# Branch norms, silu and output projection moved from the u half to the v half of a two-layer decoder trunk

## What is computed

```python
mod = (c_act @ w_ada[l] + b_ada[l])[:, None, :]
sh1, sc1, g1, sh2, sc2, g2 = jnp.split(mod, 6, axis=-1)
h = rms_norm(x) * (1.0 + sc1) + sh1
q, k, v, qi, ki, wi, cu = jnp.split(h @ w_in[l], offs, axis=-1)
attn = dsa_attention(q, k, v, qi, ki, wi).reshape(B, T, ATTN_WIDTH)   # q, k, qi, ki normed, with rope
conv = conformer_conv(cu, ...)          # GLU -> conv of 31 taps -> layer_norm -> silu
mixed = jnp.concatenate([rms_norm(attn, out_g_attn[l]), rms_norm(conv, out_g_conv[l])], axis=-1)
x = x + g1 * (mixed @ w_out[l])
h2 = rms_norm(x) * (1.0 + sc2) + sh2
# peer: q = h2 @ w_q; top 16 experts e of 16384 per token and head; coef = softmax(scores) * gelu(u[e] . h2)
x = x + g2 * sum(coef * v[e])
```

## Time and profile before

| | us |
|---|---|
| median of 3 runs | 1897.99 |
| lowest and highest | 1894.2, 1899.7 |
| the profiled execution | 1898.82 |
| its span in the trace | 1896.8 |

### The profile page before, as it was taken

How to read it: one execution, slowest core, us unless ns; L and a number is a source line. 1 busy time by engine, 2 the same in 40 slices (tenths; PEclk the granted TensorE clock), 3 DMA queues, 4 the chain that set the end, 5 groups by cost and what they waited for, 6 DMA issues and landing times.

```text
span 1896.8 us, 20984 instructions
## 1 busy us (share of the span) xinstructions
PE 1071.0 (56%) x7558; PEld 630.1 (33%) x7558; DVE 1042.1 (55%) x2867; ACT 300.3 (16%) x851; POOL 976.5 (51%) x1072
## 2 busy tenths in 40 slices
PE   3896840784786566755486555774477550003554
PEld 2584630653462115443254114453153110000110
DVE  2312399799538018888518307789728219993000
ACT  6222100243210002342100002352010000000000
POOL 2000044553355776445435677534556777776774
PEclk8897975897797667876688787986788885556887
DMA  8547798999999999999999999997999999999998
GB/s 289 176 136 267 266 369 329 382 400 343 360 336 400 409 409 402 397 388 348 401 400 402 408 409 406 399 396 277 401 405 380 409 409 410 410 410 406 407 409 321
DMA packets 230920, 696.15 MB, mean 367 GB/s; under 512 B 23958, under 2 KB 23974, under 8 KB 230818
## 3 DMA queue, kind: packets, MB, share of 16 engines
q0 software_dynamic: 148080, 538.24, 72.5%
q1 hardware_dynamic: 82738, 156.58, 22.7%
HBM read 693.70 MB, written 1.05 MB: 366 GB/s over the span
## 4 chain that ended last, share of the span: by engine, by line
DMA 40%; PE 24%; DVE 14%; POOL 11%; issue 5%; ACT 5%; POOLq 0%; ACTq 0%; DVEq 0%
DMA rows<-in_peer_v,v_at 18%; DMA rows<-in_peer_u,u_at 8%; DMA wring<-in_w_in 8%; POOL rows L517 7%; PE ps L652 6%; DVE rows L1116 6%; PE ps L599 5%; PE ps L610 5%; POOL rows L509 4%; DMA wring<-in_w_ada 4%; ACT rows L907 2%; PE ps L575 2%; PE ps L633 1%; DMA wring<-in_w_out 1%; ACT diag_eq L907 1%
## 5 line engine op out<-in xcount | busy, mean ns | idle before, releaser
L509 POOL DMA_INDIRECT rows<-in_peer_u,u_at x512 | 480.6, 939 | 585.6 <-DVE dots L1116 254.2
L1116 DVE CUSTOM_DVE_ANT_0 rows<-rows,ps 128x1024 f32<-128x1024 f32 x512 | 601.6, 1218 | 224.5 <-DMA rows<-in_peer_u,u_at 217.0
L517 POOL DMA_INDIRECT rows<-in_peer_v,v_at x512 | 484.5, 946 | 313.2 <-PE ps L652 155.4
L652 PE MATMUL ps<-rows,spread_c 128*32 128x512 f32 x2048 | 343.9, 804 | 260.8 <-DMA rows<-in_peer_v,v_at 259.6
L599 PE MATMUL ps<-wring,hT 128*128 128x512 f32 x384 | 206.0, 692 | 74.9 <-DMA wring<-in_w_in 48.3
L652 PEld LDWEIGHTS ps<-rows,spread_c 128*32 128x32 f32 x2048 | 73.8, 129 | 504.0 <-issue 500.1
L610 PE MATMUL ps<-hT,wring 128*128 128x128 f32 x1536 | 184.5, 284 | 7.3 <-ACTq L874 7.3
L610 PEld LDWEIGHTS ps<-hT,wring 128*128 128x128 f32 x1536 | 182.2, 200 | 11.2 <-ACTq L874 8.5
L599 PEld LDWEIGHTS ps<-wring,hT 128*128 128x128 f32 x384 | 81.9, 222 | 187.2 <-issue 93.9
L907 ACT ACTIVATE diag_eq<-ident,cwT 128x128 f32<-128x128 f32 x395 | 118.3, 387 | 28.9 <-PE ps L633 27.5
L548 PE MATMUL ps<-ident,coef 128*128 128x128 f32 x4 | 1.5, 373 | 192.4 <-DVE coef L1384 192.4
(11 more groups left out here) (193 smaller groups left out, 959.8 us busy)
## 6 DMA issues: line engine op xcount, KB each, us to landing
wring<-in_w_ada SPq DMA_DIRECT2D x48, 1024.0 KB, 11.4
wring<-in_w_in SPq DMA_DIRECT2D x48, 1024.0 KB, 22.3
wring<-in_peer_wq SPq DMA_DIRECT2D x32, 1024.0 KB, 12.7
wring<-in_w_out SPq DMA_DIRECT2D x16, 1024.0 KB, 19.6
rows<-in_peer_u,u_at POOLq DMA_INDIRECT x512, 12.8
rows<-in_peer_v,v_at POOLq DMA_INDIRECT x512, 9.1
wring<-in_w_in SPq DMA_DIRECT2D x4, 288.0 KB, 23.7
out_x<-xs SPq DMA_DIRECT2D x2, 512.0 KB, 4.7
```

The lines of the kernel that those rows point to most:

```text
L509: pool.indirect_dma_start(row(n), None, u_rows, bass.IndirectOffsetOnAxis(ap=u_at[:, p % 2, k:k + 1], axis=0)).then_inc(row_landed[n % SLO ...
L517: pool.indirect_dma_start(row(n), None, v_rows, bass.IndirectOffsetOnAxis(ap=v_at[:, p % 2, tok:tok + 1], axis=0)).then_inc(row_landed[n % ...
L652: ins = pe.matmul(ps[32 * g:32 * g + 32, YB + q, :], spread_c[:, g, a, :], row(n)[:, q * 512:q * 512 + 512], start=a == 0, stop=a == 31)
L1116: dve.tensor_tensor_reduce(out=row(n), in0=row(n), in1=h2_shown, scale=1.0, scalar=0.0, op0=ALU.mult, op1=ALU.add, accum_out=dots[:, k:k + ...
```

## The change

The output projection with all that leads to it goes from `first(p)` to `second(p)` on every engine. On DVE `first(p)` now ends with the division of the attention values; a new function `join(p)` at the head of `second(p)` does the conv norm (p > 0), the attention branch's norm, waits for the silu and does the conv branch's norm. For p > 0 ScalarE copies the conv bank to `hb` at the place where the silu stood, and the conv norm reads that copy. ScalarE's silu and its evacuation of `mT` come at the head of its `second`. PE takes `coefT` and the first two steps of the sums ahead of the join's turn, and has three more steps around the two output blocks and one ahead of the turn of h2; so each query block finds 4 more steps done. The order of the weight loads stays. For p = 0 the conv norm stays where it was and the order of the two branch norms is swapped.

```diff
         ada(p, "mix")
+        if p:
+            job("coefT", p - 1)
         for q in range(2):
             job("mT", p, q)
...
         ada(p, "out")
-        if p:
-            job("coefT", p - 1)
@@ PE, first(p)
-                pe.wait_ge(mixed_ready, p + 1)
-                for q in range(2):
-                    turn4(("mT", p, q), [hb[:, (4 * q + i) * P:(4 * q + i + 1) * P] for i in range(4)])
-                pe.wait_ge(mixedT_ready, 2 * (p + 1))
-                for b in range(2):
-                    proj(("out", p, b), hT)
-                ada(p, "out")
@@ PE, second(p)
-                v_to(p - 1, 1)
+                v_to(p - 1, 2)
+                pe.wait_ge(mixed_ready, p + 1)
+                for q in range(2):
+                    turn4(("mT", p, q), [hb[:, (4 * q + i) * P:(4 * q + i + 1) * P] for i in range(4)])
+                pe.wait_ge(mixedT_ready, 2 * (p + 1))
+                for b in range(2):
+                    proj(("out", p, b), hT)
+                    v_to(p - 1, 3 + b)
+                ada(p, "out")
+                v_to(p - 1, 5)
                 pe.wait_ge(h2_ready, p + 1)
...
-                v_to(p - 1, 2)
+                v_to(p - 1, 6)
...
-                    v_to(p - 1, 4 + 2 * b_)
+                    v_to(p - 1, 8 + 2 * b_)
@@ ScalarE, first(p)
                 if p:
-                    silu()
+                    act.wait_ge(conv_full, p + 1)
+                    act.copy(hb[:, AW:D], ps[:, CONV_BANK, :]).then_inc(conv_taken, 1)
...
+            def second(p):
+                l, t = divmod(p, 2)
+                act.wait_ge(silu_in, p + 1)
+                act.activation(hb[:, AW:D], hb[:, AW:D], ACT.Silu).then_inc(silu_done, 1)
                 for q in range(2):
                     evac_scaled(("mT", p, q), q, mixedT_ready, gcol)
@@ DVE, first(p)
                 if p:
-                    conv_norm()
                     more_dots(3)
...
                 if p == 0:
-                    conv_norm()
-                dve.wait_ge(silu_done, p + 1)
-                rsqrt(half_mean_square(hv, CW, gy[:, :]), 1)
-                seq_(ts(hv, hv, rs[:, 0:1], None, ALU.mult))
+                    conv_norm(0)
...
-                rsqrt(half_mean_square(ha, AW, gy[:, :]), 1)
-                seq_(ts(ha, ha, rs[:, 0:1], None, ALU.mult), mixed_ready)
@@ DVE, new; second(p) calls it first
+            def join(p):
+                if p:
+                    conv_norm(p)
+                for n, cols in enumerate((slice(0, AW), slice(AW, D))):
+                    if n:
+                        dve.wait_ge(silu_done, p + 1)
+                    rsqrt(half_mean_square(hb[:, cols], AW, gy[:, :]), 1)
+                    seq_(ts(hb[:, cols], hb[:, cols], rs[:, 0:1], None, ALU.mult), mixed_ready if n else None)
```

More of the change, by code:

```diff
@@ L987, in first @@
                         evac(("skT", p, n), skT[:, 4 * n:4 * n + 4, :].rearrange("p g n -> p (g n)"), skT_ready)
-                def silu():
-                    act.wait_ge(silu_in, p + 1)
-                    act.activation(hb[:, AW:D], hb[:, AW:D], ACT.Silu).then_inc(silu_done, 1)
                 if p:
-                    silu()
+                    act.wait_ge(conv_full, p + 1)
+                    act.copy(hb[:, AW:D], ps[:, CONV_BANK, :]).then_inc(conv_taken, 1)
                 ns = CHUNKS[t]
@@ L1014, in first @@
                 ada(p, "mix")
-                if p == 0:
-                    silu()
+            def second(p):
+                l, t = divmod(p, 2)
+                act.wait_ge(silu_in, p + 1)
+                act.activation(hb[:, AW:D], hb[:, AW:D], ACT.Silu).then_inc(silu_done, 1)
                 for q in range(2):
@@ L1019, in first @@
                 ada(p, "out")
-            def second(p):
-                l, t = divmod(p, 2)
                 for q in range(2):
@@ L1276, in first, with conv_norm @@
                         rinv[:, :].unsqueeze(2).to_broadcast([P, NH, DH]), ALU.mult), pv_taken)
-                rsqrt(half_mean_square(ha, AW, gy[:, :]), 1)
-                seq_(ts(ha, ha, rs[:, 0:1], None, ALU.mult), mixed_ready)
+            def conv_norm(p):
+                hv = hb[:, AW:D]
+                if p == 0:
+                    dve.wait_ge(conv_full, 1)
+                    o = ps[:, CONV_BANK, :]
+                else:
+                    dve.wait_ge(conv_taken, p + 1)
+                    o = hv
+                seq_(dve.bn_stats(bn6[:, :], o))
+                seq_(dve.bn_aggr(mv[:, :], bn6[:, :]))
+                rsqrt(ts(halfv[:, 0:1], mv[:, 1:2], 0.5, 0.5 * NORM_EPS, ALU.mult, ALU.add), 1)
+                seq_(ts(hv, o, mv[:, 0:1], rs[:, 0:1], ALU.subtract, ALU.mult), None if p else conv_taken)
+                seq_(tt(hv, hv, ln_gb[:, 0, :], ALU.mult))
+                seq_(tt(hv, hv, ln_gb[:, 1, :], ALU.add), silu_in)
+            def join(p):
[6 more added lines that the diff above has]
+                    seq_(ts(hb[:, cols], hb[:, cols], rs[:, 0:1], None, ALU.mult), mixed_ready if n else None)
             def best16(lists):
@@ L1363, in second @@
                 l, t = divmod(p, 2)
+                join(p)
                 dve.wait_ge(g1_ready, 2 * (l + 1))
```

## The result

| | median us | lowest, highest |
|---|---|---|
| before | 1898.85 (4 runs) | 1894.2, 1901.67 |
| after | 1870.58 (4 runs) | 1867.49, 1875.68 |

The ratio is 0.9848, with a 95% interval of 0.9831 to 0.9865: 28 us faster, where 32 were forecast (1866). A second set of runs of the changed kernel, on the chip of three experiments, gave 0.9862 (0.9827 to 0.9898). The profiled execution of after took 1869.38 us, its span 1867.6.

What follows compares the result with a forecast made beforehand. The DMA stream of gathered rows bounds from 240 us on, with DVE behind u-half holes, and a serial chain before. Gains 3.7 + 22.6 + 3.2 + 2.9 = 32.4 us off 1898.82 gave 1866; range 1852 to 1890.

Steps and rivals of the forecast that it cites:

- The holes as the only place to win: From 240 us on, time can be won only where the DMA stream is not full: 45 us within reach.
- DVE's 7.8 us in each u half: u halves, p = 1 to 3: norms moved away give back 7.8, 7.0 and 7.8 us, sum 22.6.
- p = 0: Serial chain before the first gather: division and attention norm come inside the silu wait, 3.7 us gained, bounds 2 and 4.
- what follows the coefficients: After coefficients, v half: 3.2 us gained in p = 1, 0 in p = 2, 2.9 in p = 3.
- the first projection block: Half of the output projection's pair, between steps 1 and 2 of the sums: 7.4 to 8.5 us.
- the slower rival: v half projection runs at PE's lower clock, pair 29.6 us, 13 us lost per part: 1906 us, chance 0.09.
- no change: Projection's pause takes back the u half's gain, three new holes of 9.6 us: 1898 us, chance 0.08.
- the signs of being wrong: u halves' holes keep length, stream under 300 GB/s between second and third sum in all parts, or pair over 20 us.
- The pause: v half, between steps 1 and 2 of the sums: 15 to 19 us, against 16.5 us of ring.
- Selection: Path from coefficients to h2 grows some 11 us in p = 2 and 3; PE stands 8 to 11; cost nothing.
- the margin of 3 us: Spare cover of the ring (16.5 us) over PE's stand at the turn of the expert numbers: 3 us at least.
- ScalarE at nothing: Silu and table load leave the u half, a copy of about 0.6 us replaces them: costs nothing.

Runs made afterwards that it cites:

- Experiment b: Kernel before with conv norm, silu and both branch norms left out for p = 1 to 3, PE's order kept; 1883.09 us, ratio 0.9916.
- g: Changed kernel with conv norm, silu and branch norms left out for p = 1 to 3; 1868.13 us against 1874.78 for the changed kernel beside it.
- h: Changed kernel with 14 more products (10 us) on DVE ahead of the join for p = 1 to 3; 1899.44 us, ratio 0.9988.
- e: Changed kernel without ScalarE's copy, the conv norm reading the conv's PSUM bank; 1868.09 us, ratio 0.9827 to the kernel before.
- j: Changed kernel with the join for p = 2 and 3 back late in the u half, 6 dots after the division; 1872.74 us, ratio 0.9858.
- c: Kernel before with PE's new order alone, norms and silu staying in the u half; 1893.30 us, ratio 0.9951.

## Why the prediction was right, and by how much not

*The holes as the only place to win: held.* 24.6 of 28 to 29 us are filled holes, some 22 in the second trace. The mean from the first gather on is 396 GB/s; 397 was said, and 390 was before.

*DVE's 7.8 us in each u half: held as a sum.* 7.2, 6.0 and 7.3 us against 7.8, 7.0 and 7.8; in the second trace 3.9, 7.2 and 8.6. That is 20.5 and 19.7 against 22.6. The coefficients of p = 1, said to come near 488, come at 488.0 and 492.8. Experiment b shows the cause, and that in p = 2 it needs the new order of PE, which the prediction did not see: it summed the two parts as if independent.

*p = 0: 3.0 against 3.7.* The step itself was sized right: from the silu's release to the joined block 2.8 us (173.82 to 176.58) where it was 6.5.

```profile
173.82 0.69 DVE L1079 CUSTOM_DVE_ANT_0 gy<-hb 128x512 f32<-128x512 f32 x1 [14.47 <-ACT hb L1018]
...
176.10 0.49 DVE L1285 TENSOR_SCALAR hb<-hb,rs 128x512 f32<-128x512 f32 x1
```

The block was ready 5 us earlier in all, since the silu also came 1.2 us earlier in this execution; part of it was given back further on, in a stretch that PE crossed at the lower clock (window 202 to 212, granted 0.50; 1.00 before).

*The term that was mis-sized is what follows the coefficients.* In p = 1 I charged a hole of 5 us and 2.5 was there (3.9 in the second trace), so 5.7 us gained and not 3.2. In p = 2 and 3 I charged nothing and found 1.3 and 1.6, and at 1430 to 1450, where I had 2.9 gained, 1.3. One reason is the first projection block, costed at 7.4 to 8.5 us: it took 9.76, 8.83 and 9.94, the second 7.13 each time. That speaks for the small holes of p = 2 and 3; in p = 1 the block was longer than said and the hole smaller all the same, so there the estimate of what the ring and the weights still bring was too low. The granted clock of p = 1 in the first 5 us of the first block and in the rest of it:

```profile
503.76:508.76 5.00, 5.00 (x6) 2.18 (x7) 0.00 (x0) 0.00 (x0) 0.00 (x0) 0.50 1.03 405
508.76:513.50 4.74, 4.74 (x15) 1.78 (x17) 0.00 (x0) 0.00 (x0) 0.00 (x0) 0.97 0.87 309
```

So the mechanism of the slower rival was there, but for 2 to 3 us of a block and not for all of the pair: PE got its full clock back within the first block, and 9.94 us is far from the 13 at which that rival was to decide. The Trainium skill, "TensorE: Matmul & The Clock Gate", section Why this matters for your kernels, advises against idle gaps between bursts of matmuls. The rows agree in direction: the block behind PE's waits began at the lower clock. The last section shows what they do not bear out.

The sum for *no change* has a slip: three holes of 9.6 us take back the 28.7 us won after the first gather and leave the 3.7 of p = 0, so it should have read 1895. None of the signs of being wrong appeared: the poorest of the pauses between steps 1 and 2 has 360 GB/s (379 in the first trace, p = 1), and the longest pair of blocks in the two traces takes 17.3 us without the step between them.

*The pause: held for p = 1, too long for the others.* 19.1 us in p = 1 (15 to 19 said), 12.3 in p = 2, where the join is ready before PE has its rows, and 14.2 in p = 3. That the ring just covers it is shown from both sides by g and h: some 7 us to win by having no join at all, 25 us to lose by 10 more in each.

*Selection: held, nearly.* PE reached the turn of the expert numbers of p = 3 ahead of DVE and stood, where it had 17 us of slack:

```profile
1475.37 0.48 PE L548 MATMUL ps<-ident,expert 128*128 128x128 f32 x1 [6.20 <-DVE u_at L1355]
```

6.2 us, 8 to 11 were said, and in this trace no gather was missed for it (410 GB/s from 1475 to 1505). In the second trace PE stood 7.16 us at the same place, POOL 3.17 us behind it, and the 2.1 us of the window from 1482 to 1492 are gone. So the margin of 3 us was not there every time.

*ScalarE at nothing: right as a price.* The silu of p = 1, with its table loaded at 487.99, is done before DVE ends the attention branch's norm at 497.2:

```profile
494.17 0.63 ACT L1018 ACTIVATE hb<-hb 128x512 f32<-128x512 f32 x1 [4.90 <-DVE hb L1275]
```

The copy is no part of the gain (e), which the prediction did not ask.

What stays open: why the norm from PSUM was even a little ahead of the changed kernel (their intervals overlap), and the two lengths of the tail.

## What to carry to other kernels

When a stream of transfers is the bound, measure how much of it is missing, window by window; work moved from a place where it leaves a hole to one where a ring covers it is mostly won, but only up to the ring's depth. Here some 32 us of join work went over, about 7 of them still cost, and 10 us more in each part would have undone the gain. Order matters as much as place: put what frees ring slots ahead of what waits for another engine. And read slack again after each change: the weight loads that moved took DVE's slack at the end of the u half with them (j). The worth of an edit can hang on another one: in p = 2 DVE's relief paid only together with the new order of PE (b and c).

## What was not expected of the hardware

Eleven traces here have the new order of PE, with three pairs of output blocks each. The second block of a pair took 7.13 us every time; the first, the same work, took anything from 7.13 to 10.20. PE's wait for the join right ahead of it does not decide which: without any join to wait for (g) all three first blocks took 8.83, with the new order alone (c) p = 1 took 7.13 and p = 2 and 3 took 8.83, and in p = 3 of the changed kernel, with a wait for DVE of 1.1 us in both executions, the block took 9.94 in one and 7.13 in the other. What goes with the time is the clock granted in the first 5 us of the block. The two executions of the changed kernel, p = 3, and g, p = 1:

```profile
1356.73 9.94 PE L599 MATMUL ps<-wring,hT 128*128 128x512 f32 x16 [2.10 <-ACTq L876]
1356.73:1361.73 5.00, 5.00 (x6) 2.16 (x7) 0.00 (x0) 0.00 (x0) 1.87 (x2) 0.50 1.03 408
...
1359.35 7.13 PE L599 MATMUL ps<-wring,hT 128*128 128x512 f32 x16 [2.10 <-ACTq L876]
1359.35:1364.35 5.00, 5.00 (x12) 2.37 (x13) 0.00 (x0) 0.00 (x0) 1.59 (x2) 1.00 1.03 409
...
501.51 8.83 PE L599 MATMUL ps<-wring,hT 128*128 128x512 f32 x16 [2.10 <-ACTq L876]
501.51:506.51 5.00, 5.00 (x8) 2.19 (x9) 0.00 (x0) 0.00 (x0) 3.78 (x5) 0.66 1.03 401
```

That is 0.50, 1.00 and 0.66 of full speed. Why the same kernel gets one or the other at the same place stays open.
